# Sums of squares moved into the stage before, the rounded split of the normalised x, and the first two weight tiles together

## The reference

```
h = rms_norm(x, norm1_g) * (1.0 + sc1) + sh1     # sc, sh, gate from adaLN, one set for context, one for latent
y = mixer(h @ w_in) @ w_out                      # layer 0: RWKV-7 and gated DeltaNet; layer 1: mLSTM
x = x + g1 * y
h = rms_norm(x, norm2_g) * (1.0 + sc2) + sh2
x = x + g2 * conv_ffn(h, ...)                    # u, gate = h @ w_in; (silu(conv(u)) * gate) @ w_out
```

## Time and profile before

| | |
|---|---|
| Time, median of 3 runs | 5036.11 us (5016.82 to 5044.67) |
| The profiled execution | 5028.26 us, span 5026.7 us |
| Granted TensorE clock, mean | 0.886 |
| PE busy | 4002.1 us, 80% |
| PEld busy | 3628.8 us, 72% |
| DVE busy | 2218.5 us, 44% |
| ACT busy | 1058.3 us, 21% |
| POOL busy | 956.9 us, 19% |

### The profile page before, as it was taken

How to read it: one execution, slowest core, us unless ns; L and a number is a source line. 1 busy time by engine, 2 the same in 40 slices (tenths; PEclk the granted TensorE clock), 3 DMA queues, 4 the chain that set the end, 5 groups by cost and what they waited for, 6 DMA issues and landing times. The chain is left out here.

```text
span 5026.7 us, 92676 instructions
## 1 busy us (share of the span) xinstructions
PE 4002.1 (80%) x37753; PEld 3628.8 (72%) x37753; DVE 2218.5 (44%) x3725; ACT 1058.3 (21%) x1753; POOL 956.9 (19%) x676
## 2 busy tenths in 40 slices
PE   4899667357777787376999999699398278999998
PEld 2899423146666676175999999599376278999998
DVE  2433334333333354336655565400354537465555
ACT  2100223522222343312200010201143212110001
POOL 2322000000000431022222222322011113222221
PEclk7999888678999799687999999799677589999999
DMA  3222365421111221211111111122133411111111
GB/s 124 69 91 85 126 224 179 157 68 44 53 53 43 77 84 55 94 46 30 37 47 42 42 36 40 39 89 81 34 116 98 129 34 29 42 38 43 44 42 63
DMA packets 439455, 360.46 MB, mean 72 GB/s; under 512 B 63220, under 2 KB 417709, under 8 KB 436621
## 3 DMA queue, kind: packets, MB, share of 16 engines
q1 hardware_dynamic: 427729, 287.07, 18.8%
q0 software_dynamic: 10304, 60.98, 3.0%
q10 hardware_dynamic: 1152, 8.39, 0.4%
HBM read 270.45 MB, written 85.92 MB: 71 GB/s over the span
## 5 line engine op out<-in xcount | busy, mean ns | idle before, releaser
L91 POOL TENSOR_TENSOR ffn_w_lower<-ffn_w,ffn_w_upper 128x1024 fp32r<-128x1024 f32 x168 | 404.6, 2408 | 1293.9 <-DVE ffn_w_upper L86 1293.9
L867 DVE SCALAR_TENSOR_TENSOR conv_acc<-u_tile,ffn_taps,conv_acc 128x945 f32<-128x945 f32 (+3 forms) x440 | 489.6, 1113 | 86.2 <-ACT conv_acc L825 72.2
L99 PE MATMUL ffn_ps<-HU,ffn_w_upper 128*128 128x384 f32 x2112 | 485.2, 337 | 45.5 <-POOL HL L91 45.5
L99 PE MATMUL ffn_ps<-HU,ffn_w_lower 128*128 128x384 f32 x2112 | 484.0, 337 | 0.0
L99 PE MATMUL ffn_ps<-HL,ffn_w_upper 128*128 128x384 f32 x2112 | 483.4, 336 | 0.0
L99 PEld LDWEIGHTS ffn_ps<-HU,ffn_w_upper 128*128 128x128 f32 x2112 | 378.1, 189 | 54.0 <-POOL HL L91 28.6
L99 PEld LDWEIGHTS ffn_ps<-HU,ffn_w_lower 128*128 128x128 f32 x2112 | 380.6, 190 | 0.0
L99 PEld LDWEIGHTS ffn_ps<-HL,ffn_w_upper 128*128 128x128 f32 x2112 | 379.9, 189 | 0.0
L99 PE MATMUL ffn_out_ps<-g_upper,ffn_w_upper 128*128 128x384 f32 x1056 | 354.5, 336 | 14.4 <-DVE g_lower L91 14.4
L99 PE MATMUL ffn_out_ps<-g_lower,ffn_w_upper 128*128 128x384 f32 x1056 | 354.0, 335 | 0.0
L99 PE MATMUL ffn_out_ps<-g_upper,ffn_w_lower 128*128 128x384 f32 x1056 | 353.9, 335 | 0.0
(11 more groups left out here) (458 smaller groups left out, 6758.5 us busy)
## 6 DMA issues: line engine op xcount, KB each, us to landing
ffn_w<-in_ffn_w_in_dram SPq DMA_DIRECT2D x88, 512.0 KB
ada_w<-in_ada_w_dram SPq DMA_DIRECT2D x40, 1024.0 KB, 6.9
rwkv_units<-unit_rows POOLq DMA_DIRECT2D x8, 2304.0 KB, 9.2
un<-rwkv_units SPq DMA_DIRECT2D x36, 512.0 KB, 4.3
z_even<-z_tile POOLq DMA_DIRECT2D x31, 576.0 KB, 3.1
in_w<-in_ab_w_in_dram SPq DMA_DIRECT2D x31, 512.0 KB
gun<-gdn_units SPq DMA_DIRECT2D x72, 192.0 KB, 3.7
z_odd<-z_tile POOLq DMA_DIRECT2D x24, 576.0 KB, 4.8
```

What stands on the lines that cost most here:

```text
L91: return eng.tensor_tensor(out.bitcast(F32R), x, up, ALU.subtract)
L99: mm = pe.matmul(o, w(a).bitcast(F32R), r.bitcast(F32R), start=(first and n == 0), stop=(last and n == 2))
L867: dve.scalar_tensor_tensor(out=o, in0=i, scalar=tp[:, t:t + 1], in1=o, op0=ALU.mult, op1=ALU.add).then_inc(s["conv"] if n < NCONV else s[" ...
```

## The change

The squares, their sum, Ln and Exp are made by the stage before: by adaLN for the first mixer input, by each output projection for the feed-forward behind it, by the first feed-forward for the second mixer input. rstd and the constant eps are kept for the whole program. The sum over partitions is now six fp32 matmuls, three on the sum of seven slices and three on the last square. In the norm that is left, ScalarE's shift writes the rounded upper part itself, VectorE makes the lower part as (scaled + shift) - upper, and POOL has no part in it. VectorE also makes both parts of the first two weight tiles, after two scalings and one rest. TensorE waits for both weight tiles and then gives each slice first to tile 0 and, one slice behind, to tile 1. The small tile of the mixer input is loaded as the third, cut before the last two or three tiles' steps on VectorE and split on POOL before the last stores. The loops of the output takes that make squares are written out. The core of the diff:

```diff
+def sum_squares(pe, K, s, ps, last):
+    pe.wait_ge(s["added"], KD - 2)
+    for b, i, j in BANKS:
+        pe.matmul(ps[:, b, 0:j - i], K["ones"][:], K["rstd"][:, i:j], start=True, stop=False)
+    pe.wait_ge(s["squared"], KD)
+    for b, i, j in BANKS:
+        mm = pe.matmul(ps[:, b, 0:j - i], K["ones"][:], last[:, i:j], start=False, stop=True)
+    mm.then_inc(s["summed"], 1)
...
+def norm_factor(act, K, s, ps):
+    act.wait_ge(s["summed"], 1)
+    act.activation(thirds(K["rstd"][:]), whole(ps), ACT.Ln, bias=K["eps"][:], scale=1.0 / D).then_inc(s["log"], 1)
+    act.wait_ge(s["log"], 1)
+    act.activation(K["rstd"][:], K["rstd"][:], ACT.Exp, scale=-0.5).then_inc(s["inv"], 1)
...
     def scalar(self, act):
         for k in range(KD):
             for h, (a, b) in enumerate(HALVES):
+                act.wait_ge(self.s["scaled"], 2 * k + h + 1)
+                act.activation(self.dst[0][:, k, a:b].bitcast(F32R), self.tmp[k % len(self.tmp)][:, a:b], ACT.Identity,
+                               bias=self.shift[:, k, h:h + 1]).then_inc(self.s["n_upper"], 1)
...
+        def rest(k):
+            for h, (a, b) in enumerate(HALVES):
+                dve.wait_ge(s["n_upper"], 2 * k + h + 1)
+                dve.scalar_tensor_tensor(out=self.dst[1][:, k, a:b].bitcast(F32R), in0=self.tmp[k % n][:, a:b],
+                                         scalar=self.shift[:, k, h:h + 1], in1=self.dst[0][:, k, a:b],
+                                         op0=ALU.add, op1=ALU.subtract).then_inc(s["n_lower"], 1)
+        scale(0)
+        scale(1)
+        rest(0)
+        for w in weights:
+            w()
+        for k in range(2, KD):
+            scale(k)
+            rest(k - 1)
+        rest(KD - 1)
...
+def first_tiles(pe, ps, W, X, norm):
+    for k in range(KD + 1):
+        if k < KD:
+            norm.ready(pe, k)
+        for n, c in ((0, k), (1, k - 1)):
+            if 0 <= c < KD:
+                mm = matmul_split(pe, [ps[:, n, b, 0:j - i] for b, i, j in BANKS], lambda a: W[a][:, n, c, :],
+                                  lambda a: [X[a][:, c, i:j] for _, i, j in BANKS], c == 0, c == KD - 1)
+                if c == KD - 1:
+                    yield n, mm
...
# adaLN, ScalarE: two squares behind each of the first four row copies; TensorE: the sums ahead of the last product
+                        for m in (2 * i, 2 * i + 1) if i < KD // 2 else ():
+                            if m > 2:
+                                act.wait_ge(s["added"], m - 2)
+                            square(act, K, s, m, tmp[:, m % 2])
+                    norm_factor(act, K, s, sums)
...
# output projection, VectorE
+                    for m in range(KD):
+                        take(m // 2, m % 2, m < KD - 2)
+                        if m > 1:
+                            add_square(dve, K, s, m - 1, HT[:, m - 1])
...
# first feed-forward, VectorE: at the end of each take, behind the cut
                             if more:
                                 cut(h, j + (p1 + 1))
+                            if layer == 0 and c == len(plan) - 1 and 0 < m < KD - 1:
+                                add_square(dve, K, s, m, u[:])
+                    def cut_both(h):
+                        cut(h, 0)
+                        dve.wait_ge(up[h], 1)
+                        lower(dve, WL[:, h], W[:, h], WU[:, h]).then_inc(low[h], 1)
```

More of the change, by code:

```diff
@@ L362, in _, with square @@
                     adaln_finish(link, dve, K, (0, ADA_HEAD // P), [(0, 0)])
-NORM_SEMS = ["squared", "added", "summed", "log", "inv", "scaled", "eps_set", "shifted", "n_upper", "n_lower"]
+THIRD = T // 3
+BANKS = tuple((b, b * THIRD, (b + 1) * THIRD) for b in range(3))
 HALVES = ((0, CTX), (CTX, T))
+SQ_SEMS = ["squared", "added", "summed", "log", "inv"]
+NORM_SEMS = ["scaled", "n_upper", "n_lower"]
+def square(act, K, s, m, tmp):
+    act.activation(tmp if m else K["rstd"][:], K["XT"][:, m, :], ACT.Square).then_inc(s["squared"], 1)
@@ new lines, in add_square @@
+def add_square(dve, K, s, m, tmp):
+    dve.wait_ge(s["squared"], m + 1)
+    if m > 1:
+        dve.wait_ge(s["added"], m - 1)
+    dve.tensor_tensor(K["rstd"][:], K["rstd"][:], tmp, ALU.add).then_inc(s["added"], 1)
+def sum_squares(pe, K, s, ps, last):
[6 more added lines that the diff above has]
+    mm.then_inc(s["summed"], 1)
@@ L376, in scalar @@
     def scalar(self, act):
[L377 to L384, removed]
@@ L399, in ready, with vector, scale @@
+                act.activation(self.dst[0][:, k, a:b].bitcast(F32R), self.tmp[k % len(self.tmp)][:, a:b], ACT.Identity,
+                               bias=self.shift[:, k, h:h + 1]).then_inc(self.s["n_upper"], 1)
     def ready(self, pe, k):
-        pe.wait_ge(self.s["n_lower"], k + 1)
-    def vector(self, dve):
+        pe.wait_ge(self.s["n_lower"], 2 * k + 2)
+    def vector(self, dve, weights):
         s, n = self.s, len(self.tmp)
[L404 to L415, removed]
+        def scale(k):
@@ L503, in tile @@
                         matmul_tile(pe, ps[:, k], (WU[:, k], WL[:, k]), X, KD).then_inc(mm_done[k], 1)
[L504 to L508, removed]
+                    for k in range(2):
+                        pe.wait_ge(low[k], 1)
+                    for k, mm in first_tiles(pe, ps, (WU, WL), X, norm):
+                        mm.then_inc(mm_done[k], 1)
                     with pe.Fori(0, pairs - 1) as j:
@@ L921, in _ @@
                         else:
-                            with dve.Fori(0, NM - 1) as j:
-                                take(c, p1, j, True)
-                            take(c, p1, NM - 1, False)
+                            for j in range(NM):
+                                take(c, p1, j, j < NM - 1)
                 @block.gpsimd
```

126 lines of the change are left out of this document (63 added, 63 removed).

## The result

The change is a gain, and close to the forecast. The changed kernel takes 4888.43 us in the median of four runs (4881.23 to 4901.24), the kernel before 5031.31 us in runs beside it (5016.82 to 5044.67): a ratio of 0.9717, 95% interval 0.9686 to 0.9749. The forecast was 4895 us, its range 4865 to 4955. The profiled execution took 4901.24 us (span 4899.6, granted clock 0.895), so 127.0 us less than that of before; the forecast's sum for this comparison was -137.2. By the medians the gain is 142.9 us.

What follows compares the result with a forecast made beforehand. Four stage starts of about 80.4 us were taken as bound not by PE but by the squares' chain and VectorE's slices slowed beside POOL. -172.7 - 13.2 + 6.7 + 24.0 + 18.0 = -137.2 us, so 4895 us; range 4865 to 4955.

Steps and rivals of the forecast that it cites:

- Joint first tiles: Starts of both mixer inputs and both feed-forwards: against 80.4 us each, gains of 42.7, 44.4 and twice 42.8, 172.7 us.
- The rest pair: VectorE's making of the lower part at the four starts: bounded by 1.5 and 3.9 us a pair, taken as 1.5.
- The small tile: Last tile of the two mixer inputs, cut earlier: PE runs on without idling or low clock, gaining 8.7 + 4.5 = 13.2 us.
- adaLN: Stage before the first mixer input: the moved sums, Ln and Exp make it end at 94.5, costing 6.7 us.
- The output projections: Ends of both projections: last square, sums (5.5 us) and Ln and Exp with table loads (5.05) cost 12.0 us each.
- The first feed-forward: Its end and last output tiles: 8.4 us after the last take plus 9.6 us from delayed adds, cost 18.0 us.
- The long price of the add: First feed-forward's last output tiles: POOL keeps the add out, 9.6 us lost; with the short price about 1.
- The clock did not stay low in the joint tiles: Rival for the four starts: PE's clock stays low in the joint tiles, 64.1 us more, 4959 us; chance 0.13.
- above 0.85: Sign in the trace after: granted clock at the four stage starts above 0.85.
- the clock fall in the last output tiles: Rival in the first feed-forward: PE's pauses lower its clock, seven tiles at 11.3 us, 35 us more, 4930; chance 0.05.
- The squares are hidden: Rival was that squares don't hide and three stages pay the adds' chain, some 17 us each, 4945; chance 0.03.
- The pairs were not dear: Rival at the four starts: each VectorE scale or rest pair costs 3.9 us, a loss, 5041 us; chance 0.03.

Runs made afterwards that it cites:

- e4: Changed kernel with the mixer inputs' small last tile loaded, cut and split last again, as before; 4882.17 us, ratio to the kernel before 0.9727.
- e2: Changed kernel with the norm's slices split as before: ScalarE shifts in place, VectorE rounds, POOL subtracts; 4918.17 us, ratio to the kernel before 0.9783.
- e6: Changed kernel with the first two tiles apart and the norm's lower part on POOL again; 4931.75 us, ratio to the kernel before 0.9821.
- e3: Changed kernel with squares, sums, Ln and Exp back at the start of the stage that uses them; 4927.68 us, ratio to the kernel before 0.9809.
- e5: Changed kernel with the first feed-forward's last-chunk adds moved between the next tile's second and third take; 4859.62 us, ratio to the kernel before 0.9681.
- e1: Changed kernel with TensorE finishing the first tile before it begins the second; 4891.36 us, ratio to the kernel before 0.9724.
- e7: Changed kernel with the later add, and TensorE starting slice 0 once the first tile's weights are split; 4862.09 us, ratio to the kernel before 0.9683.

## Why the prediction was right

The mechanism was right as well as the number: each term of the sum can be found in the stages.

- **Joint first tiles, 172.7.** Measured 172.35 at the third tile, and 170.2 at the fourth, to which the forecast's terms for the feed-forwards reach. The steps hold one by one: first product 8.5 forecast, 8.4 to 8.9 measured; third tile 37.7 in the first mixer input, 38.0 measured; 36.0 in the second, 37.3 (the one step that was over 1 us off); the gate tile in the feed-forward at 50.1, 50.65 measured. The 5 us at the low level of the clock were 4.9 to 6.2 here; in part that is luck, since e4's starts show 2.9 to 5.5. The rest pair, unseen before, took the cheap end of its bounds, 1.54 us, since POOL is silent in these stretches but for the third tile's weights. The dear end is seen in e2 for the pair of scalings alone, 3.94; no run has the rest pair beside POOL. The prediction did not divide this gain. e6 and e3 do: with the split and the order undone together the starts lose 68.0 us, with the squares brought back 91.6. That is 159.6 of the 170.2; the first two weight tiles, which VectorE now splits whole, no run puts back on POOL.
- **The small tile, 13.2.** From the fourth tile to the end the mixer inputs became 8.8 and 4.6 us shorter (378.2 to 369.4, 286.1 to 281.5). e4 loses 8.9 and 3.0 of it again; the 1.7 us of low clock in the second, part of the forecast's 4.5, are not lost in every run.
- **adaLN, +6.7.** Measured +7.9; Exp ends at 95.74 us, forecast 94.5, because the last row copy already ends at 90.74 where 89.5 was forecast.
- **The output projections, +12.0 each.** Measured +10.1 and +11.0, and e3 gives 10.1 and 11.1 back. Two terms were too dear. The sums took 4.1 us, not 5.5, since the clock was still high after 3.19 us of idling. And Ln's table load, which stood behind the sums in the earlier trace rows, now runs ahead of the wait for them (2251.35), which saves its 1.28 us. A likely reason is the earlier constant eps, which the prediction put at nothing: before, ScalarE waited for eps and for the sums ahead of Ln, now for the sums alone. e3, with the sums back at the start but eps still made once, has the load ahead of the wait as well (101.86, Ln at 110.76). No run changes the constant alone.
- **The first feed-forward, +18.0.** Behind the fourth tile +17.9 (797.0 to 814.9), and e3 gives 17.7 back. The adds' part, forecast 9.6 (its own working, five times 1.8 and 0.4, gives 9.4), is 10.7 by e5; the tail, forecast 8.4, is then 7.2, again with the table load ahead of the wait. The long price of the add was the right choice: five of six took 3.0 us.

That the total came within 7 us of the forecast says less than these terms do. It is partly luck, for the stages that no version touches move by up to 36 us from profile to profile.

The Trainium skill, SBUF — State Buffer, section Who interferes with whom, has a VectorE instruction with two SBUF inputs wait for a GpSimd instruction that reads SBUF and began first. The trace agrees here: an add that began 0.62 us after POOL's 2.40 us subtraction ended 1.22 us behind it, and e5's adds, clear of POOL, took 1.35.

**The rivals.** The clock did not stay low in the joint tiles: its slow stretch ends 5 to 6 us after the first product, and the windows show 0.89 to 0.91 over the two tiles. Over the whole start, with its 8.4 idle us, they show 0.80 to 0.82, so the sign of "above 0.85" came true for the tiles and not for the whole start. Nor did the clock fall in the last output tiles: TensorE's five pauses there are 1.7 us each, and the window of that end shows 0.98. The squares are hidden as far as the forecast had them hidden: the feed-forward and the projections paid the tails and the adds, and no chain of 17 us; in the projections the adds took 2.2 us in the median and TensorE waited for none but the last. The pairs were not dear: 1.54 us, against the 3.75 us from which the change would have been a loss.

**What was missed.** The profiled pair differs by 127.0 us, though the touched stages give -136.0. The rest is one stage whose code did not change: the preparation of RWKV took 356.4 us before and 366.7 after. Its lengths in the other profiles are 355.9, 356.4, 355.6, 346.4, 356.0, 345.1 and 356.6. The first 340 us of this stage, in the changed kernel and in e6 (windows, as above):

```profile
516.40:856.40 340.00, 228.48 (x862) 93.87 (x863) 136.65 (x124) 105.19 (x139) 5.34 (x10) 0.83 0.58 197
```

```profile
530.00:870.00 340.00, 239.91 (x944) 100.32 (x944) 145.18 (x134) 109.64 (x145) 5.87 (x11) 0.85 0.61 210
```

At nearly the same clock the run of the changed kernel got through 862 matmuls where e6 got through 944, with less data moved, 197 against 210 GB/s. The six profiles with some 356 us lie between, at 901 to 908 matmuls and 202 or 203 GB/s. What makes this stage jump by 10 us is open; it does not follow the change, since e1, e2, e3, e5 and e7 have it at 356 again.

## What to carry to other kernels

Where an engine waits for a chain at a stage's start, count what each producer costs per slice once the other engines are silent: here the cheap pair (1.54 instead of 3.9 us) and the joint tiles cost 39.9 and 15.2 us when undone alone, but 68.0 when undone together, so neither experiment by itself tells what its part is worth without the other. Work moved into an earlier stage is paid in that stage's tail, here 7 to 11 us for a chain that nothing covers, and in delays where it meets other work: the adds beside GpSimd's subtraction took 3.0 us instead of 1.35, and putting them behind it won back 10.7 us. Read terms of 10 us from stage lengths and tile starts, not from totals whose untouched parts move by 36 us.

## What the runs showed of the hardware that was not expected

- Ln's table load (1.28 us) ran during the wait for the sums in the changed kernel's output projection and in e3, and behind the sums in the earlier trace rows.
- The low level of the clock lasted from 2.9 to 6.2 us after TensorE's first product at starts with the same code, which moves a start by up to 1.6 us.
- After 2.80 us of idling behind the same work, TensorE went on at the high level for some 1 us in the kernel before and then fell to the low one, as the next row shows (the earlier trace rows has the first), while in e4 it stayed high. After 3.19 us, in the projection's tail, it stayed high too, and in e6 it fell behind gaps of 2.63 and 2.44 us. So the length of a gap alone does not tell whether the clock falls; what else decides is open here.

```profile
3532.15 1.17 PE L99 MATMUL in_ps<-HU,tail_w_lower 128*32 128x384 f32 x3
```
